# The head of each stage in a two-layer decoder step: TensorE's products in another order, and VectorE's first tiles in another order

## What is computed

```
h = x + 0.5 * post1(SwiGLU1(pre1(x)))            # gate/up 1024 -> 2816, down 2816 -> 1024
u = preM(h); P = u @ w_in                        # one input projection
[A | B | C | D] = conformer conv | gated linear attention | short conv | forgetting attention
h = h + postM(concat(A, B, C, D) @ w_out)
h = h + 0.5 * post2(SwiGLU2(pre2(h)))
```

## Time and profile before

| what | us |
|---|---|
| median of 3 runs | 1103.03 (1102.49 to 1106.19) |
| the profiled execution: its time | 1104.81 |
| the profiled execution: its span | 1103.0 |
| PE busy, PEld busy | 1071.3, 1035.0 |
| DVE busy, ACT busy, POOL busy | 716.0, 551.5, 221.2 |
| mean granted PE clock | 0.983 of full |

### The profile page before, as it was taken

The page is one execution under the profiler, slowest core; times in us unless marked ns, Lnnn a source line. Parts: engine busy times, 40 slices in busy tenths (PEclk is TensorE's granted clock), DMA queues, the critical chain, the costliest instruction groups (busy, mean ns, idle before and its releaser), DMA issues.

```text
span 1103.0 us, 24105 instructions
## 1 busy us (share of the span) xinstructions
PE 1071.3 (97%) x8956; PEld 1035.0 (94%) x8956; DVE 716.0 (65%) x1065; ACT 551.5 (50%) x887; POOL 221.2 (20%) x300
## 2 busy tenths in 40 slices
PE   6999999989989999999999999999898999999997
PEld 6999999888879999999999999998887899999997
DVE  5666644589995766654476665436999776666443
ACT  6544444554347644454474445446524476444542
POOL 3222211300003422220132223013000052222200
PEclk9999999989989999999999999999989899999999
DMA  7656576352626466556636555763425256565561
GB/s 274 206 178 188 171 230 215 96 159 78 211 90 195 145 190 183 176 171 185 191 128 199 187 178 178 243 185 118 138 88 181 78 176 215 185 176 183 176 180 51
DMA packets 63746, 186.92 MB, mean 169 GB/s; under 512 B 9514, under 2 KB 19762, under 8 KB 63538
## 3 DMA queue, kind: packets, MB, share of 16 engines
q1 hardware_dynamic: 63666, 185.81, 53.7%
HBM read 182.40 MB, written 3.38 MB: 168 GB/s over the span
## 4 chain that ended last, share of the span: by engine, by line
PE 94%; DVE 3%; issue 2%; ACT 1%; DMA 0%; SPq 0%; DVEq 0%; ACTq 0%
PE ub L307 19%; PE ub L309 18%; PE ub L308 18%; PE quad L308 8%; PE quad L307 8%; PE quad L309 8%; PE ub L327 2%; PE ub L328 1%; PE ub L329 1%; PE quad L327 1%; PE quad L590 1%; PE quad L329 1%; PE quad L328 1%; PE quad L589 1%; PE quad L494 1%
## 5 line engine op out<-in xcount | busy, mean ns | idle before, releaser
L285 DVE TENSOR_TENSOR w_lo<-raw,w_hi 128x1024 fp32r<-128x1024 f32 x336 | 435.8, 1302 | 331.9 <-ACT w_hi L277 331.6
L277 ACT ACTIVATE w_hi<-raw 128x1024 fp32r<-128x1024 f32 x336 | 342.8, 1026 | 277.3 <-PE ub L309 182.7
L307 PE MATMUL ub<-hg_hi,w_hi 128*128 128x264 f32 x960 | 280.1, 292 | 6.3 <-DVE proj L1275 6.3
L308 PE MATMUL ub<-hg_lo,w_hi 128*128 128x264 f32 x960 | 276.0, 287 | 0.0
L309 PE MATMUL ub<-hg_hi,w_lo 128*128 128x264 f32 x960 | 275.4, 287 | 0.0
L307 PE MATMUL ub<-act_hi,w_hi 128*128 128x264 f32 x704 | 200.5, 285 | 0.0
L309 PE MATMUL ub<-act_hi,w_lo 128*128 128x264 f32 x704 | 200.0, 284 | 0.0
L308 PE MATMUL ub<-act_lo,w_hi 128*128 128x264 f32 x704 | 199.1, 283 | 0.0
L307 PE MATMUL quad<-hg_hi,w_hi 128*128 128x264 f32 x688 | 196.4, 285 | 0.0
L307 PEld LDWEIGHTS ub<-hg_hi,w_hi 128*128 128x128 f32 x960 | 184.7, 192 | 11.0 <-DVE w_lo L285 8.7
L308 PE MATMUL quad<-hg_lo,w_hi 128*128 128x264 f32 x688 | 194.9, 283 | 0.0
(11 more groups left out here) (245 smaller groups left out, 1259.2 us busy)
## 6 DMA issues: line engine op xcount, KB each, us to landing
raw<-in_w_gu SPq DMA_DIRECT2D x176, 512.0 KB, 3.9
raw<-in_w_dn SPq DMA_DIRECT2D x64, 512.0 KB, 3.7
raw<-in_w_in SPq DMA_DIRECT2D x44, 512.0 KB, 3.9
raw<-in_w_dn SPq DMA_DIRECT2D x32, 384.0 KB, 3.5
raw<-in_w_out SPq DMA_DIRECT2D x16, 512.0 KB, 3.5
pages<-in_cache_k SPq DMA_DIRECT2D x32, 128.0 KB, 3.5
pages<-in_cache_v SPq DMA_DIRECT2D x32, 128.0 KB, 3.0
con<-in_con SPq DMA_DIRECT2D x1, 1448.0 KB
```

The lines of the kernel that those rows point to most:

```text
L277: eng.activation(w_hi[:, slot, 0:w], raw[:, slot, 0:w], ACT.Copy).then_inc(*sig("hi_ready", reps))
L285: eng.tensor_tensor(w_lo[:, slot, 0:w], raw[:, slot, 0:w], w_hi[:, slot, 0:w].bitcast(F32), ALU.subtract)\
L307: eng.matmul(out, a_hi, x_hi[:, k0 + k, :], start=(first and k == 0), stop=False)
L308: eng.matmul(out, a_hi, x_lo[:, k0 + k, :], start=False, stop=False)
```

## The change

`multiply_first` waits for the rounded tile first, does both products with `x_hi` for all three units (six matmuls), then waits for the rest and does the three products with `x_lo`. It gets the name of the rounded tile's semaphore (`hg_hi` or `ym_hi`) as one more argument. The last matmul of each unit, which signals `unit_done`, is now among the three last of the head. In `boundary` DVE's order becomes s0 a0, s1 a1, s2 r0, s3 a2 r1, s4 a3 r2, and so on to a7 r6, r7. No instruction other than waits is added or removed.

```diff
-        def multiply_first(eng, l, phase, x_hi, x_lo, banks, widths, ready, count):
+        def multiply_first(eng, l, phase, x_hi, x_lo, banks, widths, high, ready, count):
+
+            def part(w, s, k):
+                return w[:, s, k * widths[s]:(k + 1) * widths[s]]
 
             for k in range(KD):
+                eng.wait_ge(*at(l, high, count + k + 1))
                 for s in range(GROUP):
-                    m = widths[s]
                     if k == 0:
                         eng.wait_ge(S["split_done"], l * UNITS + PHASES[phase][0] + s + 1 + RING)
-                    if s == 0:
-                        eng.wait_ge(*at(l, ready, count + k + 1))
-                    a_hi, a_lo = (w[:, s, k * m:(k + 1) * m] for w in (w_hi, w_lo))
-                    out = banks[s][0:m, 0:NT]
-                    eng.matmul(out, a_hi, x_hi[:, k, :], start=k == 0, stop=False)
-                    eng.matmul(out, a_hi, x_lo[:, k, :], start=False, stop=False)
-                    mm = eng.matmul(out, a_lo, x_hi[:, k, :], start=False, stop=k == KD - 1)
+                    out = banks[s][0:widths[s], 0:NT]
+                    eng.matmul(out, part(w_hi, s, k), x_hi[:, k, :], start=k == 0, stop=False)
+                    eng.matmul(out, part(w_lo, s, k), x_hi[:, k, :], start=False, stop=False)
+                eng.wait_ge(*at(l, ready, count + k + 1))
+                for s in range(GROUP):
+                    mm = eng.matmul(banks[s][0:widths[s], 0:NT], part(w_hi, s, k), x_lo[:, k, :], start=False, stop=k == KD - 1)
                     if k == KD - 1:
                         mm.then_inc(*sig("unit_done"))
...
-                for k in range(KD + 2):
-                    if k < KD:
-                        dve.wait_ge(*at(l, "y_scaled", 8 * q + k + 1))
-                        if k >= 2:
-                            dve.wait_ge(*at(l, "h_ready", 8 * q + k - 1))
-                        dve.tensor_tensor(SCALED[k % 2], yg[:, k, :], ROOT, ALU.mult).then_inc(*sig("z_ready"))
-                    if 1 <= k <= KD:
-                        dve.wait_ge(*at(l, "z_ready", 8 * q + k))
-                        dve.tensor_tensor(resid[:, k - 1, :], resid[:, k - 1, :], SCALED[(k - 1) % 2], ALU.add)\
-                           .then_inc(*sig("h_ready"))
-                    if k >= 2:
-                        input_rest(l, q, k - 2, par[:, PAR["pre"] + 8 * q:PAR["pre"] + 8 * q + 8])
...
+                for k in range(2):
+                    scaled(k)
+                    added(k)
+                scaled(2)
+                rest(0)
+                for k in range(2, KD):
+                    if k + 1 < KD:
+                        scaled(k + 1)
+                    added(k)
+                    rest(k - 1)
+                rest(KD - 1)
```

More of the change, by code:

```diff
@@ L456, in feed_forward @@
                 pe.wait_ge(*at(l, "gu_read", f * 44))
-                multiply_first(pe, l, gu, hg_hi, hg_lo, ub, [P] * GROUP, "hg_ready", 8 * (q - 1))
+                multiply_first(pe, l, gu, hg_hi, hg_lo, ub, [P] * GROUP, "hg_hi", "hg_ready", 8 * (q - 1))
                 pe.wait_ge(setup, 16 * 3)
@@ L699, in mixer @@
             def mixer(l):
-                multiply_first(pe, l, "in", hg_hi, hg_lo, ub, IN_WIDTH, "hg_ready", 0)
+                multiply_first(pe, l, "in", hg_hi, hg_lo, ub, IN_WIDTH, "hg_hi", "hg_ready", 0)
                 pe.wait_ge(*at(l, "h_acc", 9))
@@ L710, in mixer @@
                 pe.wait_ge(*at(l, "d_pt", 4))
-                multiply_first(pe, l, "out", ym_hi, ym_lo, ub, [P] * GROUP, "ym_ready", 0)
+                multiply_first(pe, l, "out", ym_hi, ym_lo, ub, [P] * GROUP, "ym_hi", "ym_ready", 0)
                 for n in range(GROUP, KD):
@@ L986, in boundary, with scaled, added, rest @@
                     return result_tiles(l)
-                for k in range(KD + 2):
-                    if k < KD:
-                        dve.wait_ge(*at(l, "y_scaled", 8 * q + k + 1))
-                        if k >= 2:
-                            dve.wait_ge(*at(l, "h_ready", 8 * q + k - 1))
-                        dve.tensor_tensor(SCALED[k % 2], yg[:, k, :], ROOT, ALU.mult).then_inc(*sig("z_ready"))
-                    if 1 <= k <= KD:
-                        dve.wait_ge(*at(l, "z_ready", 8 * q + k))
-                        dve.tensor_tensor(resid[:, k - 1, :], resid[:, k - 1, :], SCALED[(k - 1) % 2], ALU.add)\
-                           .then_inc(*sig("h_ready"))
-                    if k >= 2:
-                        input_rest(l, q, k - 2, par[:, PAR["pre"] + 8 * q:PAR["pre"] + 8 * q + 8])
+                def scaled(k):
+                    dve.wait_ge(*at(l, "y_scaled", 8 * q + k + 1))
+                    if k >= 2:
+                        dve.wait_ge(*at(l, "h_ready", 8 * q + k - 1))
+                    dve.tensor_tensor(SCALED[k % 2], yg[:, k, :], ROOT, ALU.mult).then_inc(*sig("z_ready"))
+                def added(k):
+                    dve.wait_ge(*at(l, "z_ready", 8 * q + k + 1))
+                    dve.tensor_tensor(resid[:, k, :], resid[:, k, :], SCALED[k % 2], ALU.add).then_inc(*sig("h_ready"))
+                def rest(k):
+                    input_rest(l, q, k, par[:, PAR["pre"] + 8 * q:PAR["pre"] + 8 * q + 8])
+                for k in range(2):
[9 more added lines that the diff above has]
+                rest(KD - 1)
             def feed_forward(l, q):
```

## The result

| | before | changed |
|---|---|---|
| median of 7 runs each, us | 1104.27 | 1109.84 |
| ratio, 95% interval | | 1.0057 (1.0047 to 1.0068) |
| span of the profiled execution, us | 1103.0 | 1109.0 |

The change makes the kernel slower by 0.57%, 5.6 us on the medians and 6.0 on the spans. The forecast was 6.7, from 1103.03 to 1109.7.

What follows compares the result with a forecast made beforehand. PE, busy 97% of the span, was taken as the bound. Two "in" at 1.2, three gate/up at 1.2, two "out" at 0.2 and 0.3 for the first head sum to 6.7 us: 1103.03 becomes 1109.7, range 1102.8 to 1112.8.

Steps and rivals of the forecast that it cites:

- PE's start: Head behind a boundary: PE can start when the warm passes end, 210.61 instead of 210.91, gaining 0.30 us at most.
- DVE's first tiles and the first collision: Boundary start: a0 0.20 us earlier, POOL's first add 0.13 ahead of r0, so r0 ends at 211.30 instead of 210.76.
- The tie at tile 2: Boundary: POOL's third add leads r2 by 0.05 us and wins; r2 is held, shifting everything of DVE by 0.54.
- `unit_done` of unit 0: End of a head: signal comes 0.24 instead of 0.73 us before the end, delaying ACT's w_hi of unit 4 and the norm.
- PE's wait of 3.2 us in "in": PE at line 307 behind DVE's `proj`, once in each "in" stage: the wait gets longer by 1 us.
- "in", two: Both "in" stages: ACT's norm behind the head comes late, 221.43 against 220.21, +1.2 us each.
- gate/up behind a boundary, three: Three gate/up stages: w_lo of unit 3 ends 1.4 us later, so PE starts unit 3 late, +1.2 each.
- "out", two: Two "out" stages: unit 0 done 0.5 us later, w_lo of unit 4 also; +0.2 each, bounds 0 and 0.4.
- very first head: Kernel's first head: two more of tile 0's matmuls at the slower spacing, +0.3 us, bounds -0.5 and +0.9.
- No lasting collision: Rival at the boundaries: only r0 is held, then the old rhythm returns; +1.0 us, 1104.0; chance 0.30.
- The gain as meant: Rival at the boundaries: no collision at all, r0 ahead as well; 1102.3 to 1103 us; chance 0.08.
- C, every r held: Rival at the boundaries: 0.5 us for each of eight tiles, about 1116; chance 0.06 together with other collisions.

## Why the prediction was right

**PE's start.** The head starts when the warm passes end, not when hg_hi is there; its second matmul is at 210.81 against 211.03 before, with the boundary 0.09 later: 0.3 gained, as worked out.

**DVE's first tiles and the first collision.** a0 at 208.94 (208.86 + 0.09 forecast), the first add 0.13 ahead of r0, r0 0.90 long (0.94 forecast). Three experiments show that this is the cause: with fills in place of the adds, with the first add held back, and with DVE's old order the loss is gone, while DVE's part alone has it all.

**The tie at tile 2.** The lead was worked out as 0.05 from durations of three engines, and is 0.07 in the trace. r2 and r4 are held, r1, r3, r5, r6 are not, r7 is held at its start: the forecast tile by tile. That the lead decides, and that the rhythm keeps itself afterwards, is shown by the kernel whose third add waits.

**`unit_done` of unit 0.** The norm's lag behind the sum's product grew by 0.33 (0.65 to 0.98). The forecast has 0.36: the norm 1.22 later, the last matmul 0.86. "Out" lost 0.18 twice, forecast 0.2. Both come back with the old order in the last tile: lag 0.64, and nothing lost in "out". The norm came 1.14 late and PE started again 1.12 late in layer 0, 1.03 and 1.02 in layer 1.

**One sign was wrong.** The prediction said that PE's wait of 3.2 us in "in" would get longer by 1. It is 3.17 in all twelve traces. Only its end was thought of: PE gets to this wait from small products (line 518) that themselves wait for `proj` on the same DVE chain, so the beginning of the wait moves with the norm too. The delay is there, but it shows in when the wait ends and not in its length.

**The terms of the sum.**

| term | forecast, us | measured, us |
|---|---|---|
| "in", two | 2 x 1.2 | 1.16, 1.24 |
| gate/up behind a boundary, three | 3 x 1.2 | 0.99, 1.18, 1.00 |
| "out", two | 2 x 0.2 | 0.18, 0.18 |
| very first head | 0.3 | 0.09 |
| sum | 6.7 | 6.0 |

Two terms were too high. In the second gate/up stages w_lo of unit 3 ended at 369.84 against 367.09, with a lag of 1.43 carried in, so 1.32 later of its own; the forecast has 1.4. The rest of the difference is a misread start. I took 367.41 for the time at which PE began unit 3, and its record is 0.48 long; but the next product stands here in the kernel before:

```profile
367.72 0.28 PE L308 MATMUL quad<-hg_lo,w_hi 128*128 128x264 f32 x1
```

That is 0.31 behind, not 0.12, so PE's real start was about 367.60, and 0.2 of the 1.2 was never there. From this product to the same one after (370.13) it is 2.41, 0.98 without the lag. The 0.14 between the end of w_lo and a matmul holds: 0.17 here by the same reckoning (369.84, 370.01).

The very first head came out near its forecast by luck, as the sum of two things of which the forecast had neither at this size. PE begins the third unit 0.83 later, and its products change from 0.22 us apart to 0.12 apart 1.5 us earlier (at 16.2 against 17.7, behind the second line of the earlier trace rows). The first line is of the kernel before, the other two are of the changed one:

```profile
11.66 0.59 PE L327 MATMUL quad<-hg_hi,w_hi 128*128 128x264 f32 x1 [1.00 <-DVE w_lo L285]
...
12.49 0.59 PE L327 MATMUL quad<-hg_hi,w_hi 128*128 128x264 f32 x1 [1.23 <-DVE w_lo L285]
...
16.16 0.28 PE L327 MATMUL ub<-hg_hi,w_hi 128*128 128x264 f32 x1
```

The later w_lo is not due to the change: the kernel with VectorE's part alone, which has the old head there, has it too (its third w_lo starts at 11.11, that of the kernel before at 10.39, that of the changed one at 11.23). The change to 0.12 fell anywhere from 15.8 to 18.2 us in the twelve traces. The head's end lay between 22.0 and 23.1 us in them, and the 0.09 is no number of the change alone.

**The rivals.** "No lasting collision" was the nearest and needed the tie to fall the other way; with one wait it does. The gain as meant is there too, once the collision is out of the way, but it is given back by the late `unit_done`: 1.0010 and 1.0002 with TensorE's order complete, 0.9984 and 0.9987 with the old order in its last tile. C, every r held, did not happen: only r0, r2, r4 and r7 are.

**The w_lo that POOL holds up.** The Trainium skill ("SBUF — State Buffer", section "SBUF: two separate sides") has the loser of the shared port pair blocked for the winner's whole instruction. Here w_lo took 1.77 to 1.78 where alone it takes 1.23, with POOL 0.07 ahead: released about 0.6 us into an add of 0.76. By the whole instruction, r2 would have taken 1.18; it took 0.98, released about 0.56 into the add. The measurement decides what a held rest costs. Whether the hold is shorter than the add, or the add's record only longer than its hold, stays open: the profile calls spans on POOL rough. The same page has a GpSimd instruction that only writes not contend with such a VectorE instruction; the fills show that, all 40 rests at 0.48 to 0.49.

## What to carry to other kernels

Where two engines exclude each other, moving one by 0.3 us against the other can cost 6 us over the kernel: ask which of the two comes first at each meeting, before and after, and whether the one that wins once goes on winning. An engine that is far from busy (POOL 20%) can sit in the middle of the path in this way. If the order of such a meeting matters, fix it with a wait that costs nothing, rather than leave it to 0.05 us.

When products are reordered so that a late operand comes last, look at who waits for each product's end: the last tile can keep the old order, which was worth 1 to 2 us here. That kernel, with the first add held back, or simply with VectorE's order left alone, is the fastest one found: 0.9984 and 0.9987 of the kernel before, with intervals that end at 0.9994 and 0.9996.

## What was not expected

Two rhythms of the same code: with the same instructions on DVE and POOL, 1.08 us a tile when the rest is ahead (adds 0.94, rests 0.49) and 1.34 on the mean when the add is (adds 0.76, every second rest 0.98; 213.03 to 215.70 for two tiles). One wait of about 0.3 us in front of one add (0.35 at the first, 0.27 at the third) moves the kernel from one to the other.

The mixers of layer 0 took between 107.9 and 110.2 us in the profiled executions of different kernels that have the same code there, with a granted clock of 0.95 to 0.89; but equal clocks did not make equal times (107.9 and 109.0 us, both at 0.92), so the clock is at most part of it. One profiled span alone does not tell two kernels apart here by less than some 2 us; the marks of single stretches and the ratios of many runs do.
